# A one-core encoder step: scores put behind values, turnings put inside projections, a branch's samples gathered once, sample products in 32-column parts, and B's causal triangle added on GpSimd

## The reference

```python
for l in range(DEPTH):                                     # 2 layers
    p = split_proj(rmsnorm(x, g_norm[l]) @ w_in[l])
    o_a = dsa_prompt(qa, qi, wi, ka, va, ki)               # each query attends its top 256 keys
    o_b = fox_prompt(qb, kb, vb, jnp.cumsum(lf, axis=1))   # logits += F[t] - F[s], s <= t
    o_c = band_prompt(qc, kc, vc, c_bias[l])               # own chunk and 8 before, learned bias
    o_m = mem_attend(m_query(p), mk, mv)                   # 256 memory tokens
    x = x + merge(p, o_a, o_b, o_c, o_m, w_out[l])         # each o * silu(gate), concat, @ w_out
y_prompt = rmsnorm(x, g_final)
# the samples: the same layers, keys and values = cache (512) + own tokens
```

## Time and profile before

| | |
|---|---|
| median of 3 runs | 1946.65 us (1946.15 to 1947.08) |
| profiled execution | 1946.75 us, of which the span from first to last instruction is 1944.9 us |
| PE | 1837.4 us busy, 94% of the span |
| DVE, ACT, POOL | 1023.5, 692.2, 222.8 us busy |
| granted clock of PE, mean | 0.988 |

### The profile page before, as it was taken

How to read it: one execution, slowest core, us unless ns; L and a number is a source line. 1 busy time by engine, 2 the same in 40 slices (tenths; PEclk the granted TensorE clock), 3 DMA queues, 4 the chain that set the end, 5 groups by cost and what they waited for, 6 DMA issues and landing times.

```text
span 1944.9 us, 25479 instructions
## 1 busy us (share of the span) xinstructions
PE 1837.4 (94%) x8390; PEld 956.7 (49%) x8390; DVE 1023.5 (53%) x2741; ACT 692.2 (36%) x1657; POOL 222.8 (11%) x434
## 2 busy tenths in 40 slices
PE   7889999999999988999998899999999999799998
PEld 4434555545554444555444345555455554455543
DVE  3534656665676674332234355666666676733322
ACT  4432334323343333354223322343333333344531
POOL 1241111100000000001012411111000000000000
PEclk9999999999999999999999999999999999999999
DMA  8132333412122211112331413333221222211121
GB/s 279 56 124 94 114 117 102 156 71 75 62 101 82 87 55 49 68 43 66 109 114 57 147 65 117 125 136 109 71 93 41 100 84 87 60 48 56 55 71 43
DMA packets 56961, 174.55 MB, mean 90 GB/s; under 512 B 10288, under 2 KB 24464, under 8 KB 54272
## 3 DMA queue, kind: packets, MB, share of 16 engines
q1 hardware_dynamic: 39424, 125.85, 19.0%
q0 software_dynamic: 17408, 47.08, 7.2%
HBM read 145.91 MB, written 30.07 MB: 90 GB/s over the span
## 4 chain that ended last, share of the span: by engine, by line
PE 85%; DVE 7%; ACT 4%; issue 2%; ACTq 1%; DVEq 1%; DMA 1%; SPq 0%
PE psX L783 53%; PE psT L745 8%; PE psS L897 6%; PE psX L968 5%; DVE lower L1175 2%; PE psX L943 2%; PE psS L810 2%; PE psS L868 2%; PE psS L745 1%; ACT work L1105 1%; PE psS L908 1%; ACT work L1123 1%; DVE sc L1335 1%; PE psX L976 1%; DVE work L1394 1%
## 5 line engine op out<-in xcount | busy, mean ns | idle before, releaser
L783 PE MATMUL psX<-wring,hT 128*128 128x512 f32 (+1 forms) x2592 | 1138.6, 593 | 0.0
L783 PEld LDWEIGHTS psX<-wring,hT 128*128 128x128 f32 x2592 | 483.7, 192 | 559.1 <-issue 558.5
L1175 DVE TENSOR_SCALAR_CACHE_REDUCE lower<-sc,thr 128x640 uint8<-128x640 f32 (+5 forms) x462 | 407.3, 933 | 18.0 <-issue 9.8
L1114 ACT ACTIVATE work<-work,stat 128x256 f32<-128x256 f32 (+7 forms) x288 | 200.1, 695 | 256.0 <-DVEq L1399 252.9
L1123 ACT COPY work<-psT 128x512 f32<-128x512 f32 (+2 forms) x352 | 155.3, 483 | 92.0 <-PE psT L745 89.1
L1396 DVE CUSTOM_DVE_ANT_0 work<-psS,bias 128x640 f32<-128x640 f32 (+7 forms) x144 | 103.8, 721 | 141.5 <-PE psS L908 52.2
L745 PE MATMUL psT<-con,work 128*128 128x128 f32 x1080 | 163.8, 283 | 0.8 <-ACT work L1123 0.7
L745 PEld LDWEIGHTS psT<-con,work 128*128 128x128 f32 x1080 | 117.9, 142 | 46.4 <-issue 42.7
L745 PE MATMUL psT<-con,stage 128*128 128x128 f32 x260 | 47.2, 286 | 46.0 <-DVEq L1230 29.9
L1060 ACT COPY kv<-psX 128x256 f32<-128x256 f32 x36 | 13.4, 373 | 184.3 <-PE psX L783 184.3
L1451 POOL DMA_DIRECT2D scratch_oscr<-gate x54 | 30.3, 561 | 412.8 <-DVEq L1435 410.7
(11 more groups left out here) (202 smaller groups left out, 1722.1 us busy)
## 6 DMA issues: line engine op xcount, KB each, us to landing
wring<-in_w SPq DMA_DIRECT2D x20, 2048.0 KB, 8.5
cache<-in_kB SPq DMA_DIRECT2D x16, 512.0 KB, 4.5
cache<-in_vB SPq DMA_DIRECT2D x16, 512.0 KB, 4.0
cache<-in_kC SPq DMA_DIRECT2D x16, 512.0 KB, 4.1
cache<-in_vC SPq DMA_DIRECT2D x16, 512.0 KB, 4.1
scratch_oscr<-gate POOLq DMA_DIRECT2D x54, 128.0 KB, 2.0
hT<-scratch_oscr SPq DMA_DIRECT2D x18, 384.0 KB, 3.5
kv<-in_x SPq DMA_DIRECT2D x9, 512.0 KB, 7.0
```

Of the source, the lines that this page charges most:

```text
L783: mm = pe.matmul(X.ap(s)[:, 0:w], lhs, wv[:, kt, 0:w], start=(kt == 0), stop=(kt == KT - 1))
L1114: nc.scalar.activation(x, x, ACT.Exp, scale=-1.0, bias=stats(p)[:, 0, i:i + 1], accum_out=stats(p)[:, 1, i:i + 1]).then_inc(probs.sem, 1)
L1175: v.tensor_scalar(lower[:, at:at + STRIP_L[t]], sc[:, o], thr[:, n:n + 1], 0.0, ALU.is_lt, ALU.add, accum_out=below[:, n:n + 1])
```

## The change

`program_order()` is rewritten around a unit, and five things change with it.

1. `S` of the new pack goes first, right behind `V` of the unit before, unless the pack's tile was projected only just now ("fresh"). The work of DVE and ACT on scores becomes a step of its own, `L`, one for even and one for odd heads.
2. Where either pack has two buffers, the projection is cut: `Pa` does matmuls 0 to 2, then come `T` 1 of the pack before and `L` 1 of the new pack, then `P` does matmuls 3 to 7. `K` comes behind them.
3. `R` is done once for a branch, for all four pairs, and `om` holds all four.
4. Sample products go in four parts of 32 columns instead of two of 64, each part with one head pair's keys or values alone, so that half the products fall away. `qs` holds one pair per slot.
5. The two matmuls with the triangle are gone: POOL loads the bias rows for every prompt pack of B, waits for the load and adds the triangle to the last 128 columns.

`SPARE_UNIT` goes from 5.6 to 6.2.

```diff
-SPARE_UNIT = 5.6
+SPARE_UNIT = 6.2
...
         prev = pipe[0]
-        if prev:
-            emit("T", prev, 0)
-        turn_units()
+        fresh = pack and any(u[0][0] == pack[0] and u[1] == pack[1] for u in to_turn)
+        if fresh:
+            if prev:
+                emit("T", prev, 0)
+            turn_units()
...
-        if prev and len(buffers(prev)) == 2:
-            emit("T", prev, 1)
+        if prev and not fresh:
+            emit("T", prev, 0)
+        if pack:
+            emit("L", pack, 0)
+        turn_units()
+        if gather:
+            emit("GT", gather.pop())
         pipe.insert(0, pack)
-        old = pipe[2]
-        if old and is_sample(old):
-            emit("R", old)
-            if old[2] == PAIRS - 1:
-                gather.append(old[0])
+        if any(p and len(buffers(p)) == 2 for p in (prev, pack)):
+            odd.append((prev, pack))
+
+    def odd_heads():
+
+        if odd:
+            prev, pack = odd.pop()
+            if prev and len(buffers(prev)) == 2:
+                emit("T", prev, 1)
+            if pack and len(buffers(pack)) == 2:
+                emit("L", pack, 1)
 
     def settle():
 
-        pipe.pop()
+        odd_heads()
+        old = pipe.pop()
         if pipe[1]:
             emit("V", pipe[1])
-        if gather:
-            emit("GT", gather.pop())
+        if old and is_sample(old) and old[2] == PAIRS - 1:
+            emit("R", old[0])
+            gather.append(old[0])
 
     def project(c, t):
+        if odd:
+            emit("Pa", c, t)
+            odd_heads()
+        select(SPARE_UNIT)
         emit("P", c, t)
...
-                        for g in range(2):
-                            for r in range(2):
-                                mm = pe.matmul(o[64 * r:64 * r + 64, 0:n], qs[:, g, 64 * r:64 * r + 64],
...
+                        quarters = [(r, g, slice(64 * r + 32 * g, 64 * r + 32 * g + 32)) for r in range(2) for g in range(2)]
+                        for r, g, part in quarters:
+                            mm = pe.matmul(o[part, 0:n], qs[:, j % 2, part],
+                                           kc[r][:, g * n:(g + 1) * n] if br != "M" else
+                                           kc[0][:, (r * 2 + g) * n:(r * 2 + g + 1) * n], start=True, stop=True)
...
-                                pe.matmul(S.ap((s, hp))[:, at + plain:at + L], q[half, :], keys[half, k0 + plain:k0 + L],
-                                          start=True, stop=False)
-                            for hp in range(2):
-                                mm = pe.matmul(S.ap((s, hp))[:, at + plain:at + L], ident, con[:, C_TRI:C_TRI + P],
-                                               start=False, stop=True)
...
+                            for g in range(2):
+                                part = slice(64 * r + 32 * g, 64 * r + 32 * g + 32)
+                                mm = pe.matmul(o[part, 0:P], pT[:, b * P + part.start:b * P + part.stop],
+                                               v[:, g * P:(g + 1) * P], start=(b == 0), stop=(b == nb - 1))
...
-                    pe.matmul(X.ap(s)[32 * j:32 * j + 32, 0:W], con[:, C_SEL:C_SEL + 32], om[:, :], start=True, stop=True
-                              ).then_inc(X.fill(s).sem, 1)
+                    for g in range(2):
+                        for j in range(PAIRS):
+                            mm = pe.matmul(X.ap(s)[32 * j:32 * j + 32, g * P:(g + 1) * P],
+                                           con[:, C_SELG + 32 * g:C_SELG + 32 * g + 32], om[:, j, :], start=True, stop=True)
+                    mm.then_inc(X.fill(s).sem, 1)
...
-                for i in range(2):
-                    pool.dma_start(rows_b[:, i, 0:L], d["fp"][h0 + i:h0 + i + 1, 0:L].to_broadcast([P, L])).then_inc(pbias.sem, 16)
+                src = bass.AP(d["fp"].tensor, h0 * SEQ, [[0, P], [SEQ, n], [1, L]])
+                pool.dma_start(decays(p), src).then_inc(pbias.sem, 16)
+
+            def prompt_mask(p):
+
+                own = decays(p)[:, :, blocks(p) * P - P:]
+                pool.wait_ge(*pbias.on(p))
+                g.tensor_tensor(own, own, con[:, C_TRI:C_TRI + P].unsqueeze(1).to_broadcast([P, heads(p), P]), ALU.add
+                                ).then_inc(masked.sem, 1)
```

More of the change, by code:

```diff
@@ L282, in program_order @@
         to_norm, normed = [], []
-        while queue or pipe != [None, None] or outs or to_norm:
-            work = bool(queue) or pipe != [None, None]
+        while queue or pipe != [None, None] or gather or outs or to_norm:
+            work = bool(queue) or pipe != [None, None] or bool(gather)
             if work:
@@ L478, in encoder @@
         gmem = bias[:, 0:D]
-        rows_b = bias[:, 0:2 * D].rearrange("p (n c) -> p n c", n=2)
-        halves = bias[:, 0:2 * D].rearrange("p (h c) -> p h c", h=H)
+        rows_b = bias[:, 0:2 * D]
         strips = bias[:, 0:H * 5 * P].rearrange("p (h c) -> p h c", h=H)
@@ L586, in encoder @@
         cache_loaded = [Signal(sem(f"cache{k}_loaded"), cache_loads[k::RING], lambda u: 16 * cdmas(u)) for k in range(RING)]
-        late_b = [p for p in packs if p[1][0] == "B" and not is_sample(p[1]) and heads(p[1]) == 2]
-        last_early = packs_of("B", NT // 2 - 1)[-1]
-        halves_loaded = Signal(sem("bias_halves_loaded"), each("B"), lambda e: 16)
-        pbias = Signal(sem("prompt_bias_loaded"), late_b, lambda e: 32)
+        b_packs = [p for p in packs if p[1][0] == "B" and not is_sample(p[1])]
+        pbias = Signal(sem("prompt_bias_loaded"), b_packs, lambda e: 16)
+        masked = Signal(sem("prompt_bias_masked"), b_packs)
         strips_loaded = Signal(sem("strips_loaded"), each("C"), lambda e: 16)
@@ L596, in encoder @@
         tmask = Signal(sem("token_mask_loaded"), each("m"), lambda e: 16)
-        by_head = [(l, (p, i)) for l, p in packs for i in range(heads(p))]
+        by_head = [(l, (s[1], i)) for l, s in steps("L") for i in range(s[2], heads(s[1]), 2)]
+        begun = [(l, s[1:]) for l, s in steps("Pa")]
         logits = Signal(sem("logits_ready"), by_head)
@@ L641, in merged, with decays @@
             return gate[:, t, first * P:(first + n) * P].rearrange("p (g c) -> p g c", g=n)
+        def decays(pack):
+            n, L = heads(pack), blocks(pack) * P
+            return rows_b[:, 0:n * L].rearrange("p (h c) -> p h c", h=n)
         def tile_of(l, n):
@@ L764, in _ @@
                     mm.then_inc(S.fill(s).sem, 1)
-                elif k == "P":
+                elif k == "P" and (l, s[1:]) in begun:
+                    c, t = s[1:]
+                    wv = wring[:, chunks.index((l, c)) % 2, :].rearrange("p (k c) -> p k c", k=KT)
+                    for kt in range(3, KT):
+                        mm = pe.matmul(X.ap(s), hT[:, kt, t * P:(t + 1) * P], wv[:, kt, :], start=False, stop=(kt == KT - 1))
+                    mm.then_inc(X.fill(s).sem, 1)
+                elif k in ("P", "Pa"):
+                    s = ("P",) + s[1:]
                     c, t = s[1:]
@@ L1106, in _ @@
                     act.drain().then_inc(relued.sem, 1)
-                elif k == "S":
+                elif k == "L":
                     p = s[1]
                     L = blocks(p) * P
-                    for i in range(heads(p)):
+                    for i in range(s[2], heads(p), 2):
                         act.wait_ge(*logits.on((p, i)))
@@ L1343, in _ @@
                     dve.drain().then_inc(selected.sem, 1)
-                elif k == "S":
-                    p = s[1]
+                elif k == "L":
+                    p, hp = s[1:]
                     br, t, h0, nh = p
                     L = blocks(p) * P
-                    for i in range(heads(p)):
-                        u = (s, i % 2)
+                    for i in range(hp, heads(p), 2):
+                        u = (("S", p), hp)
                         if i < 2:
@@ L1352, in _ @@
                             n = n_pack[l, p]
-                            if i == 1 and n and len(buffers(packs[n - 1][1])) == 2 and packs[n - 1][0] == l:
-                                old = ("T", packs[n - 1][1], 1)
-                                use = (old, len(turns(packs[n - 1][1])) - 1)
-                                dve.wait_ge(*T.fill(use).on(use))
+                            if n and hp in buffers(packs[n - 1][1]):
+                                pl, old = packs[n - 1]
+                                use = (("T", old, hp), len(turns(old)) - 1)
+                                dve.wait_ge(*T.fill(use, pl).on(use, pl))
                         c = offset(p, i)
@@ L1517, in _ @@
                         pool.wait_ge(*f_dma.on("out"))
[L1518 to L1519 removed]
+                        prompt_bias(packs_of("B", 0)[0])
                         sample_bias("B", 0)
+                        prompt_mask(packs_of("B", 0)[0])
                     if c == "mm":
@@ L1658, in constants @@
     con[:, C_LEFT:C_LEFT + len(STRIPS)] = [STRIP_L[t] - STRIP_K[t] for t in STRIPS]
```

(3 more changed lines are left out.)

109 lines of the change are left out of this document (41 added, 68 removed).

## The result

The changed kernel takes 1819.37 us (median of 4 runs, 1816.28 to 1821.83) against 1946.54 us before (4 runs): a ratio of 0.9346, with a 95% interval of 0.9330 to 0.9362. The forecast was 1820 us. The profiled execution took 1821.83 us.

The account below looks back on a forecast made before the run. PE bounds the kernel, busy 1837.4 of 1944.9 us. Savings 65.5 + 6.6 + 36 + 22 + 10 = 140 us, 13 more in new waits: 1946.75 - 127 = 1820 us, range 1800 to 1842 (8 in 10: 1796 to 1870).

Parts of the forecast that it names:

- the three signs of being wrong: L970 at 0.055 us a record, PE's waits for ACT's copies over 40 us, or B's logits waiting for POOL.
- Shorter work, 65.5 us: PE's triangle, sample scores, own keys, values and gathering take 65.5 us less, after 2 us off for narrow steps.
- not four abreast: 32-column parts run only by two or their loads lie open: about 1866 us, chance 0.10.
- Changes of shape, 36 us: PE's array changes shape 406 times instead of 630; 224 fewer at 0.16 us save 36 us, ends 27 and 43.
- A2's waits, 22 of 29.9: PE's waits for DVE's rotated tile in A2 shrink by 22 of 29.9 us, ends 10 and 29.9.
- Clock, 10 us: Less time lost to PE's granted clock of 0.96 in A2's stretch: 5 us a layer, ends 0 and 15.6 in all.
- Short waits on ACT, left at 14.5: PE's short waits for ACT's copies of turnings stay at 14.5 us; ends 0 and 14.5 gained.
- New waits, 13 us: DVE late in 8 units a layer, 8 us (ends 0, 30); GT waiting for DVE's product, 5 us (ends 0, 10).
- the rival in which DVE paces: Pinned DVE order costs 1 us in each of 30 to 40 units a layer: about 1850 to 1890, chance 0.17.
- The bias, hidden: B's bias load and POOL's triangle addition, taken as 1.5 us of 1.2 to 3.9, end about when wanted.
- The rival: Slow triangle: POOL's addition at 3.9 us costs 30 to 50 us over 16 two-head packs: 1850 to 1870, chance 0.08.
- That case: B's addition from about 8 us makes the kernel slower than before; chance 0.03 for slower, 0.01 for no change.

Follow-up runs that it names:

- halves: Changed kernel with the sample products of B, C and M in two parts of 64 columns again: 1855.8 us.
- the triangle: Changed kernel with B's triangle added by PE again, GpSimd only loading the bias: 1838.2 us.
- The last run: Changed kernel with SPARE_UNIT 6.5, narrower fresh, and TR ahead of scores where T 0 fills both psT banks in B1, C1 or M1 units: 1797.6 us.
- the two moves tried: Changed kernel with SPARE_UNIT 6.5 and either GT of B, C and M behind the next V (1809.5 us) or R ahead of V (1811.9 us).
- the two runs: Changed kernel with GpSimd's triangle addition done four times (1825.4 us) or twelve times (1988.5 us) instead of once.
- The undone parts: Changed kernel with one part undone per run: late masks +14.7, no cut +70.8, turnings first +27.8, PE triangle +18.8, gathering per pair +13.7, halves +36.4 us.
- the run ahead of it: Changed kernel with SPARE_UNIT 6.5 and only units whose own turning of queries waits treated as fresh: 1810.5 us.

## Why the prediction came out, point by point

The total was right to 0.6 us in 127. That close, it was luck: the mechanisms held, but 10 us too many for changes of shape and 8 us for a lag of DVE that never came nearly cancel. The ends given for the terms add up to some 1770 to 1880 us, so the range 1800 to 1842 took it that they wouldn't all go one way. None of the three signs of being wrong showed: the sample values (L970) take 0.028 us a record in the timeline (0.035 by the group's 22.4 us for 640, which hold the change of shape too, so a little outside the sign given in busy time), PE's waits for ACT's copies are 15.6 us, and DVE's logits don't wait for POOL.

- **Shorter work, 65.5 us.** Confirmed part by part: halves cost 39.9 us of PE's time (42.7 less at most 2 predicted), the triangle 18.2 (14.2 and 16 changes of shape, 16.6). The narrow step takes 0.111 us in the timeline, the lower end, so the 2 us off for it don't show there; the 39.9 us, 2.8 under 42.7, leave that open. The rival "not four abreast" is out.
- **Changes of shape, 36 us: the mis-sized term.** The price, 0.16, was right (0.150 by the busy times, up to 0.22 at an equal clock). The count of the changed program was wrong: 24 stretches of index scores, which use two row halves, had been counted as whole array there, though not in the program before. There are 454, not 406, so 176 fewer, 26 us at 0.150. The 48 are 7 of the 9 us by which PE's busy time passed the forecast 1725.
- **A2's waits, 22 of 29.9.** 19.4; 10.5 stayed where 8 were left, and they are the one mask that the prediction named. It put no size on what the new order does by itself; with `SPARE_UNIT` back at 5.6 a third of the gain stayed.
- **Clock, 10 us.** The grant in the stretch with A2 rose from 0.96 to 0.98, not to 1.00: at most 8 us by 0.02 x 195 a layer, since part of it falls where PE stands still.
- **Short waits on ACT, left at 14.5.** 15.6. The last run shows that they could go, 11.9 us of them, for more changes of shape.
- **New waits, 13 us.** DVE's lag at `T` 1, 8 us: none; that turning has no idle time in the trace, and the rival in which DVE paces is out. `GT`: 7.9, not 5, and neither of the two moves tried took it away.
- **The bias, hidden.** Right, with the addition at half of its 1.5 us: 0.73, below the lower bound of 1.2. The rival left 2.6 us for the addition before it costs anything; the line through the two runs meets zero at 3.3. Its point of no gain, about 8 us, is 8.9 by the same line. That case was real and only its premise, a slow GpSimd, was not.

By the two sides of the span: of the 21.8 us of idle time, 6.6 of gathering waits and 19.4 in A2, less 7.9 of `GT` and 1.1 on ACT, are 17.0; the other 4.8 are small waits elsewhere, most of it PE's waits for DVE's kv, 15.0 us before (L1195) and 12.0 after (L1224), which no term had. Of the 103.1 us of busy time, 26 of shapes and up to 8 of clock leave 69 or more for shorter work, against 65.5. The 4 us between lie within what the price of a change leaves open.

The undone parts sum to 182 us with the cut in the projection, more than the change brought: the cut's 70.8 us are a loss that the new order would have made without it, and the parts share the wait in A2.

## What to carry to other kernels

Count changes of the array's shape over the whole order before and after, with every kind of matmul in its right class: here each cost 0.15 to 0.22 us, and 176 fewer, at least 26 us, were worth about as much as the faster sample values (20.6 us by their groups). When an order puts a slow step of another engine between a turning and its copy, look for the bank that the next turning wants, and put independent matmuls there. A wait that vanishes is only gained if the one that it covered (here a bank of two with three users) is gone too; run the next version and read what PE waits for now.

## What the runs showed of the hardware

- Four weight loads and matmuls into parts of 32 columns, over all rows, pass at 0.111 us a step, 0.028 a record, which is what the columns need, so the loads are hidden. By the Trainium skill, "TensorE: Matmul & The Clock Gate", section "Part 3: Packing small matmuls", under what overlaps and what doesn't, a load overlaps only if it goes to other row groups; here all four share the rows, and the trace disagrees with that sentence as it stands.
- GpSimd's addition of two float32 tensors takes 0.725 us for 256 columns and 1.27 for 512; four in a row with drains take 3.6 us, 0.9 each. The Trainium skill, "GPSIMD Engine Reference", section 4.1, has it at about twice VectorE's time; DVE's product of 256 columns (L1453, one operand in PSUM) takes 0.42 in the trace, so the factor here is 1.7 and the trace agrees.
- A short wait of PE seems to cost more than its idle time: without the cut, PE's busy time rose by 17.3 us with the same records, the same 454 changes of shape and no lower a granted clock (0.991 against 0.990). The last run points the same way: with 24 fewer waits for ACT's copies than the run ahead of it and 32 more changes of shape, PE's busy time rose by 2.0 us, not by 4.8. That the turning behind a wait shows its full 0.27 us where others follow at 0.11 would account for it; this was only argued.
